# Grouped-query attention by single heads, with the value products two items behind the scores; the depthwise convolution beside the projections

## Chip, cores and metric

One Trainium2 chip, one of its cores. The metric is the device time of one execution in microseconds (us). Everything is float32. TensorE is PE in the profile, VectorE DVE, ScalarE ACT, GpSimd POOL, SyncE SP.

## The reference

One inference step of a two-layer backbone over 512 latent tokens and 128 context tokens (640 rows, width 1024). Layer 0 mixes with an RG-LRU and differential attention, layer 1 with a gated DeltaNet and grouped-query attention; each layer ends in a mixture of 16 experts. The change lies in layer 1:

```python
z = jnp.dot(h, P['w_in_cd'][li])                     # one combined projection
qkv = jax.nn.silu(centred_depthwise_conv(qkv, conv_w))   # 4 taps, 1536 channels
q = rms_norm(qg...); k = rms_norm(kg...)             # 8 query heads, 2 key heads, 64 wide
s = jnp.einsum('bqngd,bknd->bngqk', qb, k) * HEAD_DIM ** -0.5
p = jax.nn.softmax(s, axis=-1)
o = jnp.einsum('bngqk,bknd->bqngd', p, v)
```

Latent tokens attend to 128 cached and 512 own keys (640), context tokens to their own 128.

## The kernel before

The kernel is written by hand for each engine: one program each for PE, ACT, DVE, POOL and SP, with semaphores between them. Each engine runs its program in the order in which it is written. PSUM is used as four pairs of 4 KB banks (1024 floats): `take` makes PE wait until a pair is free, `finish` marks it full, `filled` makes a reader wait for it, and `release` frees it.

Layer 1 goes as follows. PE makes the projection in six chunks (L192): two that give `z2` by rows (queries, keys, values, decay inputs), three that give the convolution's channels transposed into `pad` (four units each, `("pT", 1, c, f)`, of about 8.6 us), and one for the gate. ACT and DVE read these units in turns (`read_T`, L319); between its reads DVE normalises and rotates queries and keys (`gqa_rows_dve`). Then the decay sums follow, the queries and keys are turned (L1645 to L1652), and the attention loop starts (`gqa_pe`, `gqa_act`, `gqa_dve`).

The loop has 20 items, an item being a tile of 128 query rows and a pair of heads m; the first 16 have 640 keys, the last 4 have 128. For each item, e = 0, 1 being the two heads:

- scores on PE (L1667, L1669; L1672 in the small items): each head is 64 rows deep and uses one half of the array's rows; the orders for head 0 and head 1 alternate. Head e writes pair e. A float32 matmul shows as two in the trace.
- maximum on DVE (L1601): one reduction over both heads.
- exponential and its sum on ACT (L1517), one for each head; this frees the pair.
- reciprocal (L1608) and the product with it (L1610) on DVE.
- turn: 10 transposes on PE (L1681) into 1280 columns of pairs 2 and 3, and one copy of them on ACT (L319).
- values: 20 matmuls on PE (L1697) in two halves of the array's columns, into pair 3, and a copy of 128 columns on DVE (L1616).

PE's order is scores(j+2), turn(j+1), rows(j). DVE's is scaled(j+1), maxes(j+2), two or three of the 48 taps of the convolution (`TAPS`, L1631 and L1633), result(j). After the loop ACT runs the convolution's Silu (L2074), and PE turns the convolution's channels (`conv_pe`, L1815 and L1817); the DeltaNet follows.

Of the kernel before, what the change touches and what calls it, by code (L numbers as in the profile page):

```python
# [22 lines left out]
P = 128  # L23
# [55 lines left out]
def build(nc, io, outs):  # L79
    with ExitStack() as ctx:  # L80
# [1387 lines left out]
        upper = PSUM[:, 2:4, :].rearrange("p a b -> p (a b)")  # L1468
        gturn, gres = upper[:, 0:1280], upper[:, 1536:1664]
# [5 lines left out]
        TAPS = [(ct, tap) for ct in range(12) for tap in range(4)]  # L1475
        cv = [hflat[:, UW * i:UW * i + UW] for i in range(3)]
# [27 lines left out]
        def gqa_act(act, step):  # L1504
# [3 lines left out]
            def exps(j):  # L1508
                n = T if GP[j][0] < ST else P
                act.wait_ge(S("g_max"), j + 1)  # L1510
                if j >= 2:
                    filled(act, ("gaT", j - 2))
                if j >= 4:
                    act.wait_ge(S("g_norm"), 2 * (j - 3))
                for e in range(2):
                    u = ("gs", j, e)
                    release(act.activation(gp[j % 2][:, e, 0:n], filled(act, u)[:, 0:n], ACT.Exp, bias=nmax(j, e),  # L1517
                                           accum_out=psum_of(j, e)), u)

            def turned(j):  # L1520
                n = 2 * (T if GP[j][0] < ST else P)
                if j >= 2:
                    filled(act, ("go", j - 2))
                filled(act, ("gaT", j))
                release(copy(act, gaT[j % 2][:, 0:n], gturn[:, 0:n]), ("gaT", j))

            for j in range(-2, len(GP)):
                if j + 2 < len(GP):
                    exps(j + 2)
                if 0 <= j + 1 < len(GP):  # L1530
                    turned(j + 1)
# [53 lines left out]
        def gqa_dve(v, step):  # L1585
            filled(v, ("pR", 1, 3, 2))
            v.wait_ge(S("pad_evac0"), 8)
            v.wait_ge(S("pad_evac1"), 8)
            for c in range(3):
                for f in range(4):  # L1590
                    emptied(v, ("pT", 1, c, f))
# [3 lines left out]
            def maxes(j):  # L1595
                n = T if GP[j][0] < ST else P
                for e in range(2):
                    if j >= 4:
                        emptied(v, ("gs", j - 4, e))
                    filled(v, ("gs", j, e))  # L1600
                v.tensor_reduce(smx[:, 2 * (j % 4):2 * (j % 4) + 2], PSUM[:, 0:2, 0:n], AX_X, ALU.max, negate=True)\  # L1601
# [1019 lines left out]
```

## Time and profile before

| what | value |
|---|---|
| time, median of 3 runs | 1860.54 us (1860.17 to 1864.04) |
| the profiled execution's own time | 1863.33 us |
| its span | 1861.5 us |
| PE busy | 1578.3 us (85%) |
| DVE busy | 647.7 us (35%) |
| ACT busy | 450.9 us (24%) |
| POOL busy | 195.5 us (11%) |
| attention loop, first score to the convolution's turning | 1080.52 to 1177.19 |

Starts are in us from the span's start; a row gives the engine, the line, the tiles written and read, the shape, and the number of instructions merged in it. "Idle before" names what ended the wait.

### The profile page before, as it was taken

The numbers are of one execution on the slowest core, as the hardware profiler recorded it, in microseconds if no ns is written. First come the engines' busy times: TensorE is split into PE (matmuls) and PEld (weight loads), VectorE is DVE, ScalarE is ACT, GpSimd is POOL, SyncE is SP. The second block draws the span as 40 slices with busy tenths as digits, with TensorE's granted clock in tenths as the row PEclk, the third lists the DMA queues.
The fourth block names the chain that finished last, engine by engine and source line by source line (L and its number), as shares of the span: only waits on it lengthen the run. The fifth ranks groups of instructions, "written<-read, shape, count | busy, mean of one in ns | idle before, by whom it ended". The sixth has DMA issues, their size and how long they took to land.

```text
span 1861.5 us, 37187 instructions
## 1 busy us (share of the span) xinstructions
PE 1578.3 (85%) x16388; PEld 1039.3 (56%) x16388; DVE 647.7 (35%) x1284; ACT 450.9 (24%) x746; POOL 195.5 (11%) x197
## 2 busy tenths in 40 slices
PE   5999965778839999995999977688887957999993
PEld 2554433444517677663555456577775536667762
DVE  5134476552270000004044179734453262000003
ACT  4111284441021111103010055532221031111110
POOL 0000000000001111100000000054640001111103
PEclk8999986998969999997999989788988988999997
DMA  9822370455217999994121100000004225999994
GB/s 342 302 91 90 138 280 6 176 202 205 87 67 274 374 389 383 379 354 136 49 86 49 45 1 1 1 2 3 2 3 159 79 102 175 374 371 391 373 396 153
DMA packets 90316, 330.03 MB, mean 177 GB/s; under 512 B 10709, under 2 KB 16457, under 8 KB 82025
## 3 DMA queue, kind: packets, MB, share of 16 engines
q1 hardware_dynamic: 76016, 287.29, 40.6%
q0 software_dynamic: 9168, 32.65, 6.4%
q10 hardware_dynamic: 5032, 8.65, 1.3%
q8 instruction: 77, 1.26, 0.3%
q14 instruction: 23, 0.18, 0.0%
HBM read 303.79 MB, written 24.78 MB: 177 GB/s over the span
## 4 chain that ended last, share of the span: by engine, by line
PE 72%; DVE 12%; DMA 6%; ACT 5%; issue 5%; POOL 0%; ACTq 0%; DVEq 0%; SPq 0%
PE pairs L192 26%; PE pairs L1245 14%; PE pairs L1257 11%; DMA ring<-in_exp_w 3%; PE pairs L1228 2%; DVE sm L1601 1%; PE pairs L1934 1%; PE pairs L1936 1%; PE pairs L1923 1%; ACT arena L319 1%; PE pairs L961 1%; PE pairs L421 1%; PE pairs L1667 1%; ACT arena L1517 1%; PE pairs L1082 1%
## 5 line engine op out<-in xcount | busy, mean ns | idle before, releaser
L192 PE MATMUL pairs<-hT,ring 128*128 128x128 f32 (+1 forms) x1120 | 305.6, 436 | 2.1 <-ACT hT L319 2.1
L319 ACT ACTIVATE arena<-pairs 128x512 f32<-128x512 f32 (+7 forms) x212 | 129.8, 632 | 501.5 <-PE pairs L192 251.0
L192 PEld LDWEIGHTS pairs<-hT,ring 128*128 128x128 f32 x1120 | 170.2, 192 | 138.3 <-issue 136.8
L192 PE MATMUL pairs<-ring,hT 128*128 128x512 f32 (+1 forms) x448 | 177.4, 557 | 0.0
L1245 PEld LDWEIGHTS pairs<-arena 128*64 128x64 f32 x4096 | 145.5, 139 | 15.1 <-issue 15.0
L1245 PE MATMUL pairs<-arena 128*64 128x80 f32 x4096 | 148.3, 235 | 3.3 <-issue 2.3
L1245 PEld LDWEIGHTS pairs<-arena,ring 128*64 128x64 f32 x4096 | 142.9, 137 | 14.2 <-issue 14.2
L1245 PE MATMUL pairs<-arena,ring 128*64 128x80 f32 x4096 | 145.9, 233 | 0.9 <-issue 0.7
L192 PEld LDWEIGHTS pairs<-ring,hT 128*128 128x128 f32 x448 | 85.0, 190 | 92.0 <-issue 89.0
L1311 DVE TENSOR_SCALAR hT<-pairs,arena 80x512 f32<-80x512 f32 x32 | 23.9, 747 | 274.6 <-ACT hT L1287 274.6
L1257 PE MATMUL pairs<-ring,arena 128*80 128x512 f32 x256 | 112.8, 593 | 1.6 <-DMA ring<-in_exp_w 1.6
L1257 PE MATMUL pairs<-arena 128*80 128x512 f32 x256 | 112.6, 593 | 0.6 <-DMA arena<-in_exp_w 0.5
L1307 DVE TENSOR_TENSOR arena<-hT,pairs 128x160 f32<-128x160 f32 x64 | 20.6, 322 | 251.9 <-PE pairs L1245 251.9
L319 DVE COPY arena<-pairs 128x512 f32<-128x512 f32 (+7 forms) x37 | 25.3, 705 | 229.2 <-PE pairs L192 223.4
L1338 POOL DMA_INDIRECT moe_rows<-hT,arena x32 | 45.4, 1420 | 298.3 <-DVE hT L1311 298.3
L1257 PEld LDWEIGHTS pairs<-ring,arena 128*80 128x80 f32 x256 | 37.7, 152 | 64.6 <-issue 64.4
L1287 ACT ACTIVATE hT<-pairs,arena 80x512 f32<-80x512 f32 x32 | 21.8, 683 | 214.2 <-PE pairs L1257 214.2
L1257 PEld LDWEIGHTS pairs<-arena 128*80 128x80 f32 x256 | 37.8, 153 | 63.4 <-issue 63.4
L2334 POOL TENSOR_TENSOR arena<-ring,cst 128x256 f32<-128x256 f32 x60 | 44.0, 745 | 258.8 <-DVE ring L2233 224.0
L421 PE MATMUL pairs<-ring,late 128*32 128x512 f32 x384 | 57.1, 720 | 12.8 <-ACT arena L319 6.5
L1044 DVE SCALAR_TENSOR_TENSOR xT<-pairs,modt,xT 128x512 f32<-128x512 f32 x24 | 18.0, 750 | 141.3 <-PE pairs L192 126.5
L1278 ACT ACTIVATE arena<-pairs 128x640 f32<-128x640 f32 x32 | 22.5, 703 | 183.8 <-PE pairs L1228 183.8
(374 smaller groups left out, 2074.6 us busy)
## 6 DMA issues: line engine op xcount, KB each, us to landing
arena<-in_exp_w SPq DMA_DIRECT2D x48, 2048.0 KB, 19.2
ring<-in_exp_w SPq DMA_DIRECT2D x48, 2048.0 KB, 21.6
ring<-in_w_mod SPq DMA_DIRECT2D x24, 2048.0 KB, 8.0
ring<-in_w_in_ab SPq DMA_DIRECT2D x5, 2048.0 KB, 11.6
ring<-in_w_in_cd SPq DMA_DIRECT2D x5, 2048.0 KB, 8.1
ring<-in_w_out SPq DMA_DIRECT2D x4, 2048.0 KB, 8.0
moe_rows<-arena POOLq DMA_DIRECT2D x2, 2560.0 KB, 15.7
h_rows<-arena POOLq DMA_DIRECT2D x2, 2560.0 KB, 8.4
```

The lines of the kernel that those rows point to most:

```text
L192: last = pe.matmul(out, lhs(k), rhs(k), start=(k == 0), stop=(k == KD - 1))
L319: return eng.activation(dst, src, ACT.Copy) if eng is nc.scalar else eng.tensor_copy(dst, src)
L421: last = pe.matmul(ps[32 * q:32 * q + 32, 0:512], csil[:, k, :], w[:, k, :], start=(j == 0), stop=(j == 1))
L1228: last = pe.transpose(ps[:, o:o + CAP], xe[par][:, k::KD], ident[0:CAP, 0:CAP])
L1245: last = pe.matmul(lin_of(j, f)[c:c + 64, :], w[:, k, f * P + c:f * P + c + 64], rhs, start=(k == 0), stop=(k == KD - 1))
L1257: last = pe.matmul(PSUM[0:CAP, 3, 512 * half:512 * half + 512], hid[par][:, f, :], w2[:, f, 512 * half:512 * half + 512], start=(f == 0), ...
L1278: act.activation(xeT[par], ps, ACT.Copy).then_inc(pair_free[0], 1)
L1287: act.activation(ye[par][:, 0:512], PSUM[0:CAP, 3, 0:512], ACT.Copy, scale=gateT[:, bass.ds(i, 1)])\
L1307: v.tensor_tensor(hid[par][:, f, :], slu[par][:, f, :], lin[1][:, h], ALU.mult)\
L1311: v.tensor_scalar(ye[par][:, 512:1024], PSUM[0:CAP, 3, 512:1024], gateT[:, bass.ds(i, 1)], None, ALU.mult).then_inc(pair_free[3], 1)
L1338: g.indirect_dma_start(DR["m", l], off(e), ye[e % 2], None, compute_op=ALU.add)\
L2334: g.tensor_tensor(am64(j), a64(j), over_heads(C64[f"level{e}{s}"]), ALU.mult).then_inc(S(f"dl_am{e}"), 1)
```

## The change

- The convolution's 48 taps leave the loop: `delta_conv_dve(v, c)` runs 16 of them on DVE after `read_T` of chunk c. Its scratch tiles move from `hT` to the arena.
- The Silu leaves `delta_act`; `delta_silu_act` runs it on ACT after the three chunks' reads.
- Scores, maxima, exponentials and reciprocals go by single heads, `(j, e)`. Scores of head 1 are issued after both matmuls of head 0.
- The product with the reciprocal moves from DVE to POOL (`gqa_pool`).
- PE's order becomes scores(i, 0), scores(i, 1), rows(i-2), turn(i-1, 0), turn(i-1, 1).
- Six of the ten turned blocks go to pair 2 and are copied by ACT (768 columns); four go to the first bank of pair 3 and are copied by DVE (`rest`, 512 columns). The value products have the second bank of pair 3 (`gupper[:, 512:640]`).

```diff
 kdup = ar(20888, NT, 256)
 cdup = ar(22168, 256)
 GP = [(t, m) for t in range(NT) for m in range(4)]
-TAPS = [(ct, tap) for ct in range(12) for tap in range(4)]
-cv = [hflat[:, UW * i:UW * i + UW] for i in range(3)]
...
+def delta_conv_dve(v, c):
+    for part in range(2):
+        v.wait_ge(S("pad_evac" + str(part)), 4 + 2 * c)
+    for f in range(4):
+        emptied(v, ("pT", 1, c, f))
+    for ct in range(4 * c, 4 * c + 4):
+        for tap in range(4):
+            w = cB[:, dw_col + 12 * tap + ct:dw_col + 12 * tap + ct + 1]
+            n_tap = 4 * ct + tap
+            if n_tap:
+                v.wait_ge(S("cv_tap"), n_tap)
+            y, x = cv[ct % 2], pad[:, ct, tap:tap + UW]
+            if tap == 0:
+                v.tensor_scalar(y, x, w, None, ALU.mult).then_inc(S("cv_tap"), 1)
+            else:
+                v.scalar_tensor_tensor(out=y if tap < 3 else pad[:, ct, 0:UW], in0=x, scalar=w, in1=y,
+                                       op0=ALU.mult, op1=ALU.add).then_inc(S("cv_tap"), 1)
+def delta_silu_act(act):
+    for ct in range(12):
+        act.wait_ge(S("cv_tap"), 4 * ct + 4)
+        act.activation(pad[:, ct, 0:UW], pad[:, ct, 0:UW], ACT.Silu).then_inc(S("cv_silu"), 1)
 beta = sm[:, 256:296]
 gdec = sm[:, 296:336]
...
-    def exps(j):
+    def exps(j, e):
         n = T if GP[j][0] < ST else P
-        act.wait_ge(S("g_max"), j + 1)
-        if j >= 2:
+        act.wait_ge(S("g_max"), 2 * j + e + 1)
+        if j >= 2 and e == 1 and GP[j - 2][0] < ST:
+            act.wait_ge(S("g_rest"), j - 1)
+        elif j >= 2:
             filled(act, ("gaT", j - 2))
         if j >= 4:
-            act.wait_ge(S("g_norm"), 2 * (j - 3))
-        for e in range(2):
-            u = ("gs", j, e)
-            release(act.activation(gp[j % 2][:, e, 0:n], filled(act, u)[:, 0:n], ACT.Exp, bias=nmax(j, e),
-                                   accum_out=psum_of(j, e)), u)
+            act.wait_ge(S("g_recip"), 2 * (j - 4) + e + 1)
+        u = ("gs", j, e)
+        release(act.activation(gp[j % 2][:, e, 0:n], filled(act, u)[:, 0:n], ACT.Exp, bias=nmax(j, e),
+                               accum_out=psum_of(j, e)), u)
     def turned(j):
-        n = 2 * (T if GP[j][0] < ST else P)
+        n = 768 if GP[j][0] < ST else 256
         if j >= 2:
-            filled(act, ("go", j - 2))
-        filled(act, ("gaT", j))
-        release(copy(act, gaT[j % 2][:, 0:n], gturn[:, 0:n]), ("gaT", j))
-    for j in range(-2, len(GP)):
-        if j + 2 < len(GP):
-            exps(j + 2)
-        if 0 <= j + 1 < len(GP):
-            turned(j + 1)
+            act.wait_ge(S("g_result"), j - 1)
+        u = ("gaT", j)
+        release(copy(act, gaT[j % 2][:, 0:n], filled(act, u)[:, 256:256 + n]), u)
+    for i in range(len(GP) + 2):
+        if 0 <= i - 2 < len(GP):
+            turned(i - 2)
+        if i < len(GP):
+            exps(i, 0)
+            exps(i, 1)
...
 def gqa_dve(v, step):
-    filled(v, ("pR", 1, 3, 2))
-    v.wait_ge(S("pad_evac0"), 8)
-    v.wait_ge(S("pad_evac1"), 8)
-    for c in range(3):
-        for f in range(4):
-            emptied(v, ("pT", 1, c, f))
     for n in range(2):
         release(v.tensor_copy(gkT[:, n, :], filled(v, ("gkT", n))[:, 0:768]), ("gkT", n))
-    def maxes(j):
+    def maxes(j, e):
+        n = T if GP[j][0] < ST else P
+        if j >= 4:
+            emptied(v, ("gs", j - 4, e))
+        v.tensor_reduce(nmax(j, e), filled(v, ("gs", j, e))[:, 0:n], AX_X, ALU.max, negate=True)\
+            .then_inc(S("g_max"), 1)
+    def recip(j, e):
+        emptied(v, ("gs", j, e))
+        if j >= 4:
+            v.wait_ge(S("g_norm"), 2 * (j - 4) + e + 1)
+        v.reciprocal(rsum(j, e), psum_of(j, e)).then_inc(S("g_recip"), 1)
+    def rest(j):
+        if GP[j][0] < ST:
+            if j >= 2:
+                v.wait_ge(S("g_result"), j - 1)
+            v.wait_ge(S("g_rest"), j + 1)
+            v.tensor_copy(gaT[j % 2][:, 768:1280], gupper[:, 0:512]).then_inc(S("g_rest_read"), 1)
+    def result(j):
+        t, m = GP[j]
+        v.wait_ge(S("g_result"), j + 1)
+        v.tensor_copy(hT[:, 4 + m, t * P:t * P + P], gupper[:, 512:640]).then_inc(S("g_result_read"), 1)
+    for i in range(len(GP) + 3):
+        if 0 <= i - 1 < len(GP):
+            recip(i - 1, 0)
+        if 0 <= i - 2 < len(GP):
+            rest(i - 2)
+        if 0 <= i - 3 < len(GP):
+            result(i - 3)
+        if 0 <= i - 1 < len(GP):
+            recip(i - 1, 1)
+        if i < len(GP):
+            maxes(i, 0)
+            maxes(i, 1)
+def gqa_pool(g):
+    for j in range(len(GP)):
         n = T if GP[j][0] < ST else P
         for e in range(2):
-            if j >= 4:
-                emptied(v, ("gs", j - 4, e))
-            filled(v, ("gs", j, e))
-        v.tensor_reduce(smx[:, 2 * (j % 4):2 * (j % 4) + 2], PSUM[:, 0:2, 0:n], AX_X, ALU.max, negate=True)\
-            .then_inc(S("g_max"), 1)
-    def scaled(j):
-        n = T if GP[j][0] < ST else P
-        for e in range(2):
-            emptied(v, ("gs", j, e))
-        step(v.reciprocal(rsum(j, 0, 2), psum_of(j, 0, 2)))
-        for e in range(2):
-            v.tensor_scalar(gp[j % 2][:, e, 0:n], gp[j % 2][:, e, 0:n], rsum(j, e), None, ALU.mult)\
-                .then_inc(S("g_norm"), 1)
-    def result(j):
-        t, m = GP[j]
-        filled(v, ("go", j))
-        release(v.tensor_copy(hT[:, 4 + m, t * P:t * P + P], gres), ("go", j))
-    for j in range(-2, len(GP)):
-        if 0 <= j + 1 < len(GP):
-            scaled(j + 1)
-        if j + 2 < len(GP):
-            maxes(j + 2)
-        for ct, tap in TAPS[(j + 2) * len(TAPS) // 22:(j + 3) * len(TAPS) // 22]:
-            w = cB[:, dw_col + 12 * tap + ct:dw_col + 12 * tap + ct + 1]
-            n_tap = 4 * ct + tap
-            if n_tap:
-                v.wait_ge(S("cv_tap"), n_tap)
-            c, x = cv[ct % 2], pad[:, ct, tap:tap + UW]
-            if tap == 0:
-                v.tensor_scalar(c, x, w, None, ALU.mult).then_inc(S("cv_tap"), 1)
-            else:
-                v.scalar_tensor_tensor(out=c if tap < 3 else pad[:, ct, 0:UW], in0=x, scalar=w, in1=c,
-                                       op0=ALU.mult, op1=ALU.add).then_inc(S("cv_tap"), 1)
-        if j >= 0:
-            result(j)
+            g.wait_ge(S("g_recip"), 2 * j + e + 1)
+            p = gp[j % 2][:, e, 0:n]
+            g.tensor_tensor(p, p, rsum(j, e).broadcast_to((P, n)), ALU.mult).then_inc(S("g_norm"), 1)
...
-    def scores(j):
+    def scores(j, e):
         t, m = GP[j]
-        ps = [take(pe, ("gs", j, e), e) for e in range(2)]
-        q = [gqT[64 * e:64 * e + 64, m, t * P:t * P + P] for e in range(2)]
-        k = [gkT[64 * e:64 * e + 64, m // 2, :] for e in range(2)]
+        u = ("gs", j, e)
+        ps = take(pe, u, e)
+        r = slice(64 * e, 64 * e + 64)
+        q, k = gqT[r, m, t * P:t * P + P], gkT[r, m // 2, :]
         if t < ST:
-            for e in range(2):
-                pe.matmul(ps[e][:, 0:512], q[e], k[e][:, 0:512], start=True, stop=True)
-            for e in range(2):
-                finish(pe.matmul(ps[e][:, 512:T], q[e], k[e][:, 512:T], start=True, stop=True), ("gs", j, e))
+            pe.matmul(ps[:, 0:512], q, k[:, 0:512], start=True, stop=True)
+            finish(pe.matmul(ps[:, 512:T], q, k[:, 512:T], start=True, stop=True), u)
         else:
-            for e in range(2):
-                finish(pe.matmul(ps[e][:, 0:P], q[e], k[e][:, T:768], start=True, stop=True), ("gs", j, e))
-    def turn(j):
-        pe.wait_ge(S("g_norm"), 2 * j + 2)
+            finish(pe.matmul(ps[:, 0:P], q, k[:, T:768], start=True, stop=True), u)
+    def turn(j, e):
+        nk = NT if GP[j][0] < ST else 1
+        pe.wait_ge(S("g_norm"), 2 * j + e + 1)
         u = ("gaT", j)
-        take(pe, u, 2)
-        nk = NT if GP[j][0] < ST else 1
-        for e in range(2):
-            for b in range(nk):
-                last = pe.transpose(gturn[:, (e * nk + b) * P:(e * nk + b + 1) * P],
-                                    gp[j % 2][:, e, b * P:b * P + P], ident)
-        finish(last, u)
+        ps = take(pe, u, 2) if e == 0 else PSUM[:, 2, :]
+        for b in range(nk):
+            k = e * nk + b
+            if k == 6 and j:
+                pe.wait_ge(S("g_rest_read"), j)
+            out = ps[:, 256 + P * k:384 + P * k] if k < 6 else gupper[:, P * (k - 6):P * (k - 5)]
+            ins = pe.transpose(out, gp[j % 2][:, e, b * P:b * P + P], ident)
+            if k == (5 if nk == NT else 1):
+                finish(ins, u)
+            elif k == 9:
+                ins.then_inc(S("g_rest"), 1)
     def rows(j):
         t, m = GP[j]
         nk = NT if t < ST else 1
-        u = ("go", j)
-        take(pe, u, 3)
+        if j:
+            pe.wait_ge(S("g_result_read"), j)
         emptied(pe, ("gaT", j))
+        if nk == NT:
+            pe.wait_ge(S("g_rest_read"), j + 1)
         o = 64 * (m // 2)
         for b in range(nk):
             vals = z2[:, ST, 656 + o:720 + o] if t == ST else \
                 gv_c[:, o:o + HD] if b == 0 else z2[:, b - 1, 656 + o:720 + o]
             for e in range(2):
-                last = pe.matmul(gres[64 * e:64 * e + 64, :], vals,
+                last = pe.matmul(gupper[64 * e:64 * e + 64, 512:640], vals,
                                  gaT[j % 2][:, (e * nk + b) * P:(e * nk + b + 1) * P], start=(b == 0),
                                  stop=(b == nk - 1))
-        finish(last, u)
+        last.then_inc(S("g_result"), 1)
     pe.wait_ge(pair_free[3], units.uses[3])
-    for j in range(-2, len(GP)):
-        if j + 2 < len(GP):
-            scores(j + 2)
-        if 0 <= j + 1 < len(GP):
-            turn(j + 1)
-        if j >= 0:
-            rows(j)
+    for i in range(len(GP) + 2):
+        if i < len(GP):
+            scores(i, 0)
+            scores(i, 1)
+        if 0 <= i - 2 < len(GP):
+            rows(i - 2)
+        if 0 <= i - 1 < len(GP):
+            turn(i - 1, 0)
+            turn(i - 1, 1)
+    pe.wait_ge(S("g_result_read"), len(GP))
...
 def delta_act(act, step):
-    def silu(ct):
-        act.wait_ge(S("cv_tap"), 4 * ct + 4)
-        act.activation(pad[:, ct, 0:UW], pad[:, ct, 0:UW], ACT.Silu).then_inc(S("cv_silu"), 1)
-    for ct in range(8):
-        silu(ct)
     for c in range(4):
         emptied(act, ("cvT", c))
     act.activation(heads5(qsq), heads4(dq), ACT.Square).then_inc(S("qk_sq"), 1)
-    for ct in range(8, 12):
-        silu(ct)
     for c in range(4, 8):
         emptied(act, ("cvT", c))
     act.activation(heads5(ksq), heads4(dk), ACT.Square).then_inc(S("qk_sq"), 1)
...
@@ -2483,6 +2506,7 @@
             for c in range(3):
                 gqa_rows_act(act, step, c)
                 read_T(act, 1, c, pad[:, 4 * c:4 * c + 4, :], 0, True)
+            delta_silu_act(act)
             read_gate(act, 0)
             filled(act, ("pR", 1, 3, 2))
             decay_act(act)
@@ -2536,6 +2560,7 @@
                 else:
                     gqa_rows_dve(v, step, c)
                 read_T(v, 1, c, pad[:, 4 * c:4 * c + 4, :], 1, True)
+                delta_conv_dve(v, c)
             read_gate(v, 1)
             decay_sums_dve(v, step)
             gqa_dve(v, step)
@@ -2559,6 +2584,7 @@
     route_pool(g, 0)
     moe_pool(g, 0)
     layer1_outputs(g)
+    gqa_pool(g)
     delta_pool(g, step)
     route_pool(g, 1)
     moe_pool(g, 1)
```

## Rows read from the trace of the kernel before

**Rows 1.** The page: its chain, shares by engine.
```profile
PE 72%; DVE 12%; DMA 6%; ACT 5%; issue 5%; POOL 0%; ACTq 0%; DVEq 0%; SPq 0%
```

**Rows 2.** Windows of the loop: stretch, length, busy by engine, granted clock, DMA.
```profile
1080.50:1091.27 10.77, 6.17 (x27) 4.05 (x27) 7.24 (x10) 3.47 (x9) 0.00 (x0) 0.68 0.00 0
...
1115.53:1159.48 43.95, 34.58 (x342) 26.30 (x343) 39.81 (x66) 25.09 (x46) 0.00 (x0) 1.00 0.00 1
...
1168.30:1177.19 8.89, 4.12 (x27) 2.01 (x27) 8.60 (x20) 4.62 (x14) 0.00 (x0) 0.70 0.00 1
```

**Rows 3.** Waits from 1080 to 1177: us in total, times, longest.
```profile
ACT arena L1517 <- DVE sm L1601: 43.4, 19, 5.3
```

**Rows 4.** The critical chain in the loop: start, us, what.
```profile
1080.52 1.13 PE pairs L1667 x4
...
1091.27 1.13 PE pairs L1667 x4
...
1115.53 1.13 PE pairs L1667 x4
...
1117.03 1.50 DVE sm L1601
...
1120.35 1.13 PE pairs L1667 x4
...
1159.48 0.51 PE pairs L1672 x4
```

**Rows 5.** PE's timeline in two items: start, length, line, operation.
```profile
1116.81 1.31 PE L1681 MATMUL pairs<-cst,arena 128*128 128x128 f32 x10
1118.06 0.44 PE L1697 MATMUL pairs<-arena,late 128*64 128x128 f32 x4
...
1165.92 0.44 PE L1697 MATMUL pairs<-arena,late 128*64 128x128 f32 x4
...
1167.16 0.49 PE L1672 MATMUL pairs<-arena 64*128 64x128 f32 x4
```

**Rows 6.** PE's timeline in the projection's last chunk.
```profile
1032.22 34.50 PE L192 MATMUL pairs<-ring,hT 128*128 128x512 f32 x80
```

**Rows 7.** Groups by shape, 960 to 1240 us: count, busy us, mean ns, idle before.
```profile
L1601 DVE TENSOR_REDUCE sm<-pairs 128x2 f32<-128x1280 f32 x16 | 23.9, 1491 | 7.0 <-PE pairs L1669 7.0
...
L1601 DVE TENSOR_REDUCE sm<-pairs 128x2 f32<-128x256 f32 x4 | 1.7, 422 | 0.0
...
L1517 ACT ACTIVATE arena<-pairs,sm 128x640 f32<-128x640 f32 x32 | 25.1, 789 | 38.8 <-DVE sm L1601 38.8
...
L319 ACT ACTIVATE arena<-pairs 128x1280 f32<-128x1280 f32 x16 | 19.8, 1234 | 0.5 <-PE pairs L1681 0.5
...
L1616 DVE COPY hT<-pairs 128x128 f32<-128x128 f32 x20 | 5.7, 285 | 1.3 <-PE pairs L1697 1.3
...
L319 DVE COPY arena<-pairs 128x512 f32<-128x512 f32 x6 | 4.2, 692 | 69.2 <-PE pairs L192 69.2
...
L1633 DVE SCALAR_TENSOR_TENSOR hT<-arena,cB,hT 128x643 f32<-128x643 f32 x24 | 21.2, 884 | 0.4
```

**Rows 8.** Groups by shape on POOL, whole span.
```profile
L2345 POOL TENSOR_TENSOR ring<-arena,sm 128x512 f32<-128x512 f32 x9 | 9.3, 1038 | 15.2 <-PE pairs L1999 12.1 <-PE pairs L1989 3.1
...
L1446 POOL TENSOR_TENSOR arena<-arena,xT 128x1024 f32<-128x1024 f32 x2 | 6.4, 3199 | 0.2
```

**Rows 9.** DVE's timeline beside the projection.
```profile
964.00 2.81 DVE L777 TENSOR_REDUCE sm<-arena 128x40 f32<-128x2560 f32 x1
...
983.87 0.89 DVE L319 COPY arena<-pairs 128x512 f32<-128x512 f32 x2
...
997.81 0.89 DVE L319 COPY arena<-pairs 128x512 f32<-128x512 f32 x2 [13.06 <-PE pairs L192]
```

**Rows 10.** Timeline where the loop ends.
```profile
1175.10 1.28 ACT L2074 ACT_TABLE_LOAD   x1
...
1177.19 1.98 PE L1815 MATMUL pairs<-cst,arena 128*64 128x128 f32 x16 [0.87 <-ACT arena L2074]
```

More of the change, by code:

```diff
@@ L1467, in build @@
         gaT = [ar(20888 + 1280 * i, 1280) for i in range(2)]
-        upper = PSUM[:, 2:4, :].rearrange("p a b -> p (a b)")
-        gturn, gres = upper[:, 0:1280], upper[:, 1536:1664]
+        gupper = PSUM[:, 3, :]
         gscr = ar(18328, NT * 8, HD)
@@ L1473, in build @@
         GP = [(t, m) for t in range(NT) for m in range(4)]
-        TAPS = [(ct, tap) for ct in range(12) for tap in range(4)]
-        cv = [hflat[:, UW * i:UW * i + UW] for i in range(3)]
+        cv = [ar(14232 + UW * i, UW) for i in range(2)]
+        def delta_conv_dve(v, c):
[19 more added lines that the diff above has]
+                act.activation(pad[:, ct, 0:UW], pad[:, ct, 0:UW], ACT.Silu).then_inc(S("cv_silu"), 1)
         beta = sm[:, 256:296]
@@ L1821, in conv_read @@
             u = ("cvT", ct)
-            filled(eng, ("go", len(GP) - 1))
+            eng.wait_ge(S("g_result"), len(GP))
             eng.wait_ge(S("caches"), 80)
@@ L2411, in layer1_ready @@
         def layer1_ready(pe):
-            emptied(pe, ("go", len(GP) - 1))
+            pe.wait_ge(S("g_result_read"), len(GP))
             for b in range(4):
```

## The prediction

> **What bounds the kernel now.** I read the page's chain first: the end is set by PE for 72% of the span and by DVE for 12% [rows 1]. The change touches the projection of layer 1, where PE streams without a gap, and the attention loop, so the question is who sets the loop's pace. In the windows of its steady part PE is busy 34.58 of 43.95 us, DVE 39.81, ACT 25.09, POOL never, and the granted clock is 1.00 [rows 2]. The waits say that ACT's exponentials stood 43.4 us for DVE's maximum [rows 3]. The chain shows the circle: an item's scores start at 1115.53, the maximum of both heads follows at 1117.03 for 1.50 us, then the two exponentials, and the next item's scores start at 1120.35 because both pairs must be free [rows 4]. One round is 4.82 us. It is a latency circle: PE stands idle for about 1 us of it, and DVE fills its gaps with the taps.
>
> From the start of item 2's scores (1091.27) to item 16's (1159.48) there are 14 rounds in 68.2 us, 4.87 each. Before them items 0 and 1 took 10.75 us from 1080.52 [rows 4] at a mean clock of 0.68 [rows 2]. After them, 17.7 us pass from 1159.48 to the first turning of the convolution at 1177.19 [rows 4, 10].
>
> **The change, part by part.** All pieces are put into one round whose time zero is the start of head 0's scores.
>
> *PE.* The turn takes 1.25 us from its start to the start of the values (1116.81 to 1118.06), and the values 1.24 us to the start of the next scores (1165.92 to 1167.16) [rows 5]. Both remain. The scores change. Before, they took 1.28 us (1115.53 to 1116.81) [rows 4, 5]. Alone, one pass over 512 columns takes 34.50 / 80 = 0.431 us [rows 6], so four passes for the two heads would take 1.72 us, and the four short ones of 128 columns 0.43 us: 2.16 us. Before, the heads alternated and ran side by side in the two halves of the array, which is why 1.28 was enough. Now both matmuls of head 0 stand ahead of head 1's first in PE's order, and they use the same half. I count 2.16 us, plus 0.15 for the start and the change of shape (1.28 exceeds half of 2.16 by 0.20; the estimate keeps most of it), less 0.11 for head 1's first pass beside head 0's last: 2.2 us. The sum of PE's round is 2.2 + 1.24 + 1.25 = 4.69 us. Bounds: 3.8 if the heads still ran side by side, 4.9 if nothing overlaps and each further semaphore costs something.
>
> The row shows four passes and the short ones in 1.28 us when the heads alternate [rows 4, 5], less than four times the 0.431 us of a pass [rows 6]. The Trainium skill (TensorE: Matmul & The Clock Gate, Part 3: Packing small matmuls, The mechanism) says that matmuls keep program order and only those in other row groups overlap. By it the new order gives the 2.2 us; were it not so, 1.28 would stay and the round would be 3.8 us. This rule speaks against the new order.
>
> *DVE.* Two maxima of 640 columns: the rows at 1280 and 256 columns differ by 1069 ns for 1024 columns [rows 7], so one is 0.82 us. Copying 512 columns of the turn takes 0.69, the result 0.285 [rows 7], and two reciprocals a little: with 0.3 for these, 2.9 us a round. The two multiplications and the taps (48 of them, 0.884 us for most [rows 7], some 38 us in all) are gone. DVE no longer sets the pace.
>
> *ACT.* Two exponentials at 0.79 each, and a copy that shrinks from 1280 columns, 1.23 us [rows 7], to 768, some 0.8: 2.4 us. Not the pace.
>
> *POOL.* A product of 640 columns with a broadcast factor. The nearest row is 1038 ns for 512 columns with a broadcast operand, so 1.30 us; with two full operands it is 3199 ns for 1024, so 2.0 us [rows 8]. I take 1.30, since the operand is broadcast here too. Two are 2.6 us a round (4.0 at most), below 4.69. POOL would set the pace from 2.35 us for one.
>
> The multiplication on DVE was cheaper than on POOL. The Trainium skill (GPSIMD Engine Reference, 3.1 Elementwise — side-by-side cycle accounting) measures 4497 ns for 2048 columns of two operands; by it one product is an estimated 1.4 us and a round's two are 2.8 us. It speaks against the move, but changes no sum here.
>
> *Does PE find everything ready?* Head 0's scores end at 1.1 and head 1's at 2.2. The maxima run from 1.3 to 2.1 and from 2.4 to 3.2, the exponentials from 2.2 to 3.0 and from 3.3 to 4.1. The next round starts at 4.69, and both pairs are free: the circle that set 4.82 is down to about 3.1 for each head. The values of item i-2 start at 2.2; their blocks were turned by time 0 and copied by ACT and DVE by about 1.0. The latest piece is the product of head 1: its reciprocal waits on DVE behind `rest` and `result` until 1.3, POOL multiplies until about 2.8, and PE wants it at 2.2 + 1.24 + 0.62 = 4.06. That is 1.3 us of slack, 0.6 with the dearer product. So I take the steady round as PE's 4.69: 14 x (4.87 - 4.69) = 2.5 us gained. With the bounds 3.8 and 4.9 it is from 15 us gained to 0.4 lost.
>
> *Start of the loop.* Head 0's first exponential ends at 3.0 and head 1's at 4.1; scores of item 1 fill 3.1 to 5.4, the turn of item 0 follows, and item 2 starts at 6.9, if the clock is full. With half the clock from the second item on, which the 0.68 suggests [rows 2], it is 9.8. Gain 0.9 to 3.9 us; I take 1.0, the clock being as before.
>
> *End of the loop.* Item 16's round still holds a full value product and turn: 3.4 us with a wait for the last full product. The next waits for the copies of that turn, 1.1, then 1.24 and 0.3: 2.65. Two rounds of small items follow at about 1.6 and 1.8, then the last product, its turn, copy, values and result: about 4.0. That is 13.4 us with the 0.70 clock of this stretch [rows 2] in mind, against 17.7: 4.3 gained (3 to 5.5). In it is ACT's table load and first Silu, which PE waited 0.87 us for [rows 10]; the new wait for the last result costs about 0.5 in its place.
>
> *The convolution beside the projection.* PE is busy without a break there [rows 6], and DVE mostly waits for it: 13.06 us before one read [rows 9]. 16 taps are 12.8 us. Chunk 0's taps start at 964.0, where the query rows' work began, and that work (964.00 to 983.87 [rows 9]) then ends at 997. DVE's first read of chunk 1 slips from 983.87 to 997. The pair it frees is wanted again only three units after it was filled, at about 1006 (filled by 980.5, each unit 8.6 us by 34.50 / 4 [rows 6]). Cover: 9 us. Chunk 1's taps run from 998.7 to 1011.5 and delay the keys' rows to about 1023, while PE projects until 1066.7; chunk 2's end by 1046, when the gate's first unit fills (two of five tiles of the 34.50 us from 1032.22 [rows 6]). ACT's 12 Silus go under the same cover. Cost: nothing; if a chunk's taps took over 22 us the surplus would be paid by PE.
>
> *After the loop.* The turning of the convolution is paced by PE and DVE's copies as before. No gain, no loss, except for the clock.
>
> **Sum.** 1.0 + 2.5 + 4.3 = 7.8 us. The profiled execution took 1863.33 us (span 1861.5), 2.8 over the median 1860.54; taken from the median the forecast is 1852.7 us.
>
> **Rivals.**
>
> *The heads overlap after all.* PE's round is then 3.8, and the other engines' longest circle is below it. For it: they did overlap; against: the order. 14 x 1.07 + 5.3 = 20 us gained: about 1840. Chance 0.06.
>
> *Nothing gained in the steady part.* PE's round is 4.87 or more, because the serial scores, changes of shape and added waits eat the idle 1 us. For it: my 4.69 is only 0.18 below what is there. Only start and end are left, 5.3 us or less: 1855 to 1860. Chance 0.20, of which half lies within 0.2%.
>
> *POOL sets the pace (the slower side).* From 2.35 us a product POOL is the bound. Against: 1.04 us for 512 columns [rows 8]. At twice the broadcast row's rate, 2.6 us, a round is 5.4 with the hand-overs: 16 x 0.53 = 8.5 lost against 5.3 gained, 1864; with more, later. Chance 0.05.
>
> *The taps stall the projection.* DVE frees a pair too late and PE stands still. Against: 9 us of cover. Were a chunk's taps to take twice their 12.8 us, 4 us beyond the cover would be lost in each of two chunks, and the whole comes to about no change, 1861. Chance 0.03.
>
> **How the numbers follow.** The forecast has 0.66, its own range 1848 to 1857, from the start's 0.9 to 3.9, the round between 4.6 and 4.8 and the end's 3 to 5.5. The range of 8 in 10 reaches into the second rival and some way toward the first: 1845 to 1859. 0.2% is 3.7 us, about what a measurement of this kernel can tell from no change. Faster: 0.66 + 0.06 + 0.10 = 0.82; within: 0.10 + 0.03 = 0.13; slower: 0.05.
>
> **What the new profile would show.** Scores of a full item last about 2.2 us from start to the start of the values; the steady round is 4.6 to 4.8 us with PE busy over 95% of it; ACT's wait for the maximum no longer lengthens the round; POOL's products are about 1.3 us; DVE has the taps between 964 and 1047, and the projection ends at 1066.8 as before; the loop starts at 1080.5 and the turning of the convolution at about 1169. I would be wrong if the products took over 2.35 us, if scores took 1.3 us, or if PE showed gaps before L192 or before the turn.

## The result and the profile after

The changed kernel takes 1843.8 us (median of 4 executions, 1838.64 to 1847.48) against 1862.3 us for the kernel before in the same comparison. The ratio is 0.990 with a 95% interval of 0.987 to 0.993: 18.5 us less. The forecast was 1852.7 us with a range of 1845 to 1859, so the direction was right and the gain more than twice the 7.8 us foretold.

The profiled execution took 1838.64 us, the fastest of the four, and its span is 1836.1 us, 25.4 less than that of the profile before. Where they lie:

| stretch | before | after | difference |
|---|---|---|---|
| span's start to the projection's end | 1066.8 | 1064.3 | -2.5 |
| projection's end to the first score | 13.8 | 11.5 | -2.3 |
| first score to item 2's scores | 10.8 | 8.7 | -2.0 |
| 14 full rounds, items 2 to 15 | 68.2 | 55.2 | -13.0 |
| item 16's scores to the convolution's turning | 17.7 | 12.6 | -5.2 |
| from there to the span's end | 684.3 | 683.8 | -0.5 |

The first line holds the projection beside which the taps now run, but the projection takes 177.3 us in both kernels (889.45 to 1066.72 before, 886.96 to 1064.23 after), so its 2.5 us lie ahead of it. In the second line the mean clock differs: 0.83 from 1060 to 1080.5 before, 1.00 from 1060 to 1075.75 after. This stretch took 11.4 to 13.8 us in the kernels below, and 11.6 in b_scores_by_head, whose program is the old one there. So I read the change as the loop's 20.2 us, which agrees with the 18.5 of the medians.

The windows of the changed kernel, with the columns of [rows 2]:

```profile
1075.75:1084.49 8.74, 6.95 (x28) 4.85 (x28) 3.60 (x7) 3.97 (x9) 3.71 (x3) 0.71 0.00 0
...
1100.00:1134.00 34.00, 34.00 (x335) 27.32 (x335) 23.15 (x53) 20.38 (x44) 22.14 (x18) 1.00 0.01 2
...
1143.39:1152.27 8.88, 6.42 (x58) 3.98 (x57) 4.55 (x20) 4.41 (x17) 2.79 (x7) 0.94 0.00 1
```

PE is busy in all 34.00 us of the middle window, where it was busy 34.58 of 43.95 [rows 2]. DVE has fallen from 39.81 of 43.95 to 23.15 of 34.00. The chain, set out like [rows 4], now stays on PE through whole rounds:

```profile
1104.67 1.16 PE pairs L1689 x4
1105.83 0.36 PE pairs L1690 x3
1106.19 1.24 PE pairs L1726 x20
1107.44 1.24 PE pairs L1706 x10
1108.68 1.07 PE pairs L1689 x4
...
1109.97 1.24 PE pairs L1726 x20
1111.21 1.24 PE pairs L1706 x10
1112.45 1.16 PE pairs L1689 x4
```

L1689 and L1690 are the scores, L1726 the values, L1706 the turn. Values and turn take 1.24 us each, as foretold. The scores take 1.52 and 1.29 us in turns, not 2.2, and the rounds 4.00 and 3.77 us. Both kinds stand in PE's timeline:

```profile
1112.38 1.37 PE L1689 MATMUL pairs<-arena 64*128 64x512 f32 x4
...
1113.34 0.63 PE L1690 MATMUL pairs<-arena 64*128 64x128 f32 x4
...
1113.90 0.44 PE L1726 MATMUL pairs<-arena,late 128*64 128x128 f32 x4
...
1116.39 1.14 PE L1689 MATMUL pairs<-arena 64*128 64x512 f32 x4
...
1117.35 0.40 PE L1690 MATMUL pairs<-arena 64*128 64x128 f32 x4
...
1117.68 0.44 PE L1726 MATMUL pairs<-arena,late 128*64 128x128 f32 x4
```

Four passes over 512 columns in 1.14 us can't be one behind the other: a single one takes 0.431 [rows 6]. In the longer kind head 1's first pass starts 0.25 us after head 0's, because its pair was still in use: the second exponential of the item before ends 0.20 us after head 0's start. The groups by shape give the pieces, as in [rows 7]:

```profile
L1658 POOL TENSOR_TENSOR arena<-arena,sm 128x640 f32<-128x640 f32 x32 | 40.0, 1252 | 85.8 <-DVE sm L1625 85.8
...
L1541 ACT ACTIVATE arena<-pairs,sm 128x640 f32<-128x640 f32 x32 | 25.1, 790 | 29.2 <-DVE sm L1618 29.2
L1618 DVE TENSOR_REDUCE sm<-pairs 128x1 f32<-128x640 f32 x32 | 25.0, 819 | 8.6 <-PE pairs L1690 8.6
...
L319 ACT ACTIVATE arena<-pairs 128x768 f32<-128x768 f32 x16 | 12.9, 807 | 1.2 <-PE pairs L1706 1.2
```

The forecast had 1.30 for the product on POOL, 0.82 for a maximum, 0.8 for the copy; they are 1.25, 0.82 and 0.81.

Beside the projection, DVE's timeline (first row) and PE's (second):

```profile
1041.73 2.74 DVE L1492 SCALAR_TENSOR_TENSOR arena<-arena,cB 128x643 f32<-128x643 f32 x3
```
```profile
1029.73 34.50 PE L192 MATMUL pairs<-ring,hT 128*128 128x512 f32 x80
```

The last taps end at about 1044.4, when DVE begins to read the gate's first unit, and the last chunk still takes 34.50 us [rows 6], the whole projection still 177.3: the taps cost the projection nothing.

### The profile page after: what moved, and what is told of

Same layout as the page of the kernel before. It is cut to its first block, busy times and chain, and to the rows that moved or that the text cites. A ratio compares the mean times of both kernels' runs of the same rounds, so it can differ in the third digit from the quotient of the medians.

```text
span 1836.1 us, 37283 instructions
## 1 busy us (share of the span) xinstructions
PE 1571.6 (86%) x16388; PEld 1039.0 (57%) x16388; DVE 645.6 (35%) x1300; ACT 444.5 (24%) x746; POOL 238.5 (13%) x237
## 4 chain that ended last, share of the span: by engine, by line
PE 75%; DVE 11%; DMA 6%; issue 4%; ACT 4%; POOL 0%; ACTq 0%; DVEq 0%; SPq 0%
PE pairs L192 26%; PE pairs L1245 14%; PE pairs L1257 11%; DMA ring<-in_exp_w 3%; PE pairs L1228 2%; PE pairs L1965 1%; PE pairs L1967 1%; PE pairs L421 1%; PE pairs L1706 1%; PE pairs L1726 1%; PE pairs L1954 1%; PE pairs L1689 1%; PE pairs L961 1%; ACT arena L319 1%; PE pairs L1082 1%
## 5 line engine op out<-in xcount | busy, mean ns | idle before, releaser
L319 ACT ACTIVATE arena<-pairs 128x512 f32<-128x512 f32 (+6 forms) x212 | 122.8, 600 | 452.3 <-PE pairs L192 201.6
L1245 PEld LDWEIGHTS pairs<-arena,ring 128*64 128x64 f32 x4096 | 142.7, 137 | 13.8 <-issue 13.8
L192 PEld LDWEIGHTS pairs<-ring,hT 128*128 128x128 f32 x448 | 84.8, 190 | 92.2 <-issue 89.1
L421 PE MATMUL pairs<-ring,late 128*32 128x512 f32 x384 | 53.0, 674 | 14.6 <-ACT arena L319 5.9
L501 ACT ACTIVATE arena<-xT 128x640 f32<-128x640 f32 x32 | 23.4, 736 | 154.6 <-DVE xT L1047 135.2
## 6 DMA issues: line engine op xcount, KB each, us to landing
ring<-in_w_in_ab SPq DMA_DIRECT2D x5, 2048.0 KB, 11.5
```

The lines of the kernel that those rows point to most:

```text
L192: last = pe.matmul(out, lhs(k), rhs(k), start=(k == 0), stop=(k == KD - 1))
L319: return eng.activation(dst, src, ACT.Copy) if eng is nc.scalar else eng.tensor_copy(dst, src)
L421: last = pe.matmul(ps[32 * q:32 * q + 32, 0:512], csil[:, k, :], w[:, k, :], start=(j == 0), stop=(j == 1))
L501: act.activation(sq_all[:, k, :] if (l, n) == (1, 0) else sq[:, k % 2, :], xT[:, k, :], ACT.Square).then_inc(S("sq"), 1)
L1245: last = pe.matmul(lin_of(j, f)[c:c + 64, :], w[:, k, f * P + c:f * P + c + 64], rhs, start=(k == 0), stop=(k == KD - 1))
```

## The experiments

All loops below are measured in the profile from the first score to the first turning of the convolution. "Round" is the usual length of a full round; two numbers alternate. Ratios are to the kernel before.

| kernel | round, us | loop, us | median, us | ratio (95%) |
|---|---|---|---|---|
| before | 4.82 | 96.7 | 1862.3 | 1 |
| changed | 3.77, 4.00 | 76.5 | 1843.8 | 0.990 (0.987 to 0.993) |
| b_scores_by_head | 4.84 | 97.6 | 1864.6 | 1.001 (0.999 to 1.003) |
| a_one_half | 4.84 | 94.7 | 1859.3 | 0.998 (0.996 to 0.999) |
| a_three_blocks | 4.30 | 85.0 | 1848.5 | 0.992 (0.989 to 0.995) |
| a_five_blocks | 4.57 | 89.1 | 1851.5 | 0.995 (0.993 to 0.996) |
| b_conv_beside | 4.82 | 93.1 | 1861.3 | 1.000 (0.998 to 1.001) |
| b_conv_and_pool | 5.56 | 109.3 | 1874.1 | 1.006 (1.004 to 1.008) |
| a_heads_alone | 4.96, 5.30 | 102.5 | 1864.7 | 1.002 (1.000 to 1.004) |
| a_taps_in_loop | 3.89, 4.23 | 85.7 | 1853.7 | 0.995 (0.993 to 0.996) |
| a_product_dve | 3.94, 4.02 | 78.3 | 1841.6 | 0.988 (0.986 to 0.991) |
| a_product_twice | 4.84 | 92.8 | 1858.4 | 0.998 (0.997 to 0.999) |
| a_values_last | 3.81, 4.12 | 78.3 | 1840.1 | 0.989 (0.986 to 0.992) |
| a_result_first | 3.77, 4.01 | 76.2 | 1842.4 | 0.989 (0.987 to 0.991) |

Names with b_ start from the kernel before, those with a_ from the changed one. Medians of one comparison run some 2 us beside those of another (the kernel before had 1861.9 to 1863.8), so the ratios and the loops carry the argument.

**What do the scores cost in the new order?**

b_scores_by_head:

```diff
                     for e in range(2):
                         pe.matmul(ps[e][:, 0:512], q[e], k[e][:, 0:512], start=True, stop=True)
-                    for e in range(2):
                         finish(pe.matmul(ps[e][:, 512:T], q[e], k[e][:, 512:T], start=True, stop=True), ("gs", j, e))
```

> The kernel before, with head 1's scores issued only after both matmuls of head 0; nothing else. Theory A (the two halves of the array run side by side whatever the order of issue): scores still 1.28 us from their start to the turn's, round 4.82 us, time unchanged within 2 us. Theory B (the premise of the prediction: this order makes the heads run one behind the other): scores 2.2 us, the circle of 4.82 us grows by 0.9, and 16 rounds cost 14 us more.

PE's timeline has the scores from 1113.66 to the turn at 1114.95, 1.29 us, as before:

```profile
1113.66 1.14 PE L1667 MATMUL pairs<-arena 64*128 64x512 f32 x4 [0.63 <-ACT arena L1517]
1114.59 0.42 PE L1668 MATMUL pairs<-arena 64*128 64x128 f32 x4
1114.95 0.77 PE L1680 MATMUL pairs<-cst,arena 128*128 128x128 f32 x5
```

Theory A holds: the loop is 0.9 us longer and the median 0.8. The premise of the forecast, that this order makes the heads run one behind the other, is false already on the kernel before.

a_one_half (head 1's scores come from head 0's rows, so the attention output differs from the reference's):

```diff
-                r = slice(64 * e, 64 * e + 64)
+                r = slice(0, 64)
```

> The changed kernel, with head 1's scores taken from head 0's rows, so that both heads need the same half of the array (its attention output is therefore not the reference's). Both theories: the scores can't overlap, 2.2 us, and PE's round becomes the 4.69 us of the prediction. Theory A: the round goes from 3.9 to 4.7 us, 14 rounds cost 11 us, time near 1855 us. Theory B: nothing changes, since the heads were serial already and the gain came from elsewhere.

```profile
1120.07 1.12 PE L1689 MATMUL pairs<-arena 64*128 64x512 f32 x2
1121.03 0.38 PE L1690 MATMUL pairs<-arena 64*128 64x128 f32 x2
1121.25 1.02 PE L1689 MATMUL pairs<-arena 64*128 64x512 f32 x2
1122.11 0.38 PE L1690 MATMUL pairs<-arena 64*128 64x128 f32 x2
1122.42 0.44 PE L1726 MATMUL pairs<-arena,late 128*64 128x128 f32 x4
```

Now the heads do follow one another: 2.35 us from 1120.07 to 1122.42, and the round is 4.84. Theory A, but at a higher price than expected: the loop is 18.2 us longer than the changed kernel's, 17.1 in the 14 full rounds where 11 were foretold. Of these 4.5 lie in the first round alone (9.22 against 4.68 us), which ran at a granted clock of 0.50 here and of 0.80 in the changed kernel. This is the world that the forecast described; its 4.69 was 0.15 low, and the kernel is 4.5 us faster than before by the medians.

a_five_blocks and a_three_blocks ask how far behind head 1 may stand:

```diff
-                    pe.matmul(ps[:, 0:512], q, k[:, 0:512], start=True, stop=True)
-                    finish(pe.matmul(ps[:, 512:T], q, k[:, 512:T], start=True, stop=True), u)
+                    for b in range(NT):
+                        last = pe.matmul(ps[:, b * P:b * P + P], q, k[:, b * P:b * P + P], start=True, stop=True)
+                    finish(last, u)
```

> The changed kernel with each head's scores in five matmuls of 128 columns in place of one of 512 and one of 128: ten short passes of head 0 stand ahead of head 1's first. Theory A (PE lets the other half of the array start however far behind it stands in the order): scores 1.3 to 1.6 us, round 3.9 us, no change within 2 us. Theory C (it looks only a few passes ahead): head 1 starts late, scores 1.8 to 2.3 us, round 4.4 to 4.8 us, 7 to 12 us lost.

```profile
1109.77 2.16 PE L1690 MATMUL pairs<-arena 64*128 64x128 f32 x20
...
1111.86 0.44 PE L1727 MATMUL pairs<-arena,late 128*64 128x128 f32 x4
```

The scores take 2.09 us for the same columns, and the round 4.57: theory C. By the single starts in the trace, head 1's first pass starts 0.78 us after head 0's first, when seven of head 0's ten passes have started. With one matmul of 512 and one of 128 it starts at once, when one of four has. In both, three passes of head 0 had not started. Its pair is not what it waits for: the exponential that frees it ended 0.56 us ahead of head 0's first pass. The first full round, at a granted clock of 0.50, took 8.53 us, and the loop is 12.6 us longer than the changed kernel's. The next kernel takes 256, 256 and 128 columns, six passes:

```diff
-                    pe.matmul(ps[:, 0:512], q, k[:, 0:512], start=True, stop=True)
+                    pe.matmul(ps[:, 0:256], q, k[:, 0:256], start=True, stop=True)
+                    pe.matmul(ps[:, 256:512], q, k[:, 256:512], start=True, stop=True)
```

> The changed kernel with each head's scores in matmuls of 256, 256 and 128 columns: six passes of head 0 ahead of head 1's first. In the two kernels so far head 1 started when three passes of head 0 had not started. If that is the rule here (theory C): head 1 starts with head 0's third pass, 0.45 us in, scores 1.7 us, every full round 4.2 to 4.25 us, 4 to 5 us lost. Rival (the look-ahead goes by columns or by time, and 640 columns lie within it as before): head 1 starts at once, round 3.9 us, nothing lost.

```profile
1111.33 0.70 PE L1689 MATMUL pairs<-arena 64*128 64x256 f32 x2
1111.86 0.38 PE L1690 MATMUL pairs<-arena 64*128 64x256 f32 x1
1111.87 0.48 PE L1689 MATMUL pairs<-arena 64*128 64x256 f32 x1
...
1112.29 0.38 PE L1691 MATMUL pairs<-arena 64*128 64x128 f32 x2
1112.40 0.59 PE L1690 MATMUL pairs<-arena 64*128 64x256 f32 x2
1112.83 0.38 PE L1691 MATMUL pairs<-arena 64*128 64x128 f32 x2
1113.14 0.44 PE L1727 MATMUL pairs<-arena,late 128*64 128x128 f32 x4
```

L1689 is the first block, L1690 the second, L1691 the last. Head 0's two passes of L1689 come at 1111.33, its third pass at 1111.86, and head 1's first at 1111.87, ahead of three of head 0's that stand before it in the program. Here too the pair was free, 0.33 us ahead of head 0's first pass. The scores take 1.81 us and the round is 4.30, 0.05 above the range. The rule of three held; the sum of the loss did not. The loop is 8.5 us longer than the changed kernel's where 4 to 5 were foretold, 3.2 of it in the first full round (7.84 against 4.68 us), at a granted clock of 0.52.

**Which part gains?**

b_conv_beside: `delta_conv_dve` and `delta_silu_act` in the kernel before, the taps out of its loop.

```diff
-                for ct, tap in TAPS[(j + 2) * len(TAPS) // 22:(j + 3) * len(TAPS) // 22]:
...
+                        delta_conv_dve(v, c)
...
+                    delta_silu_act(act)
```

> The kernel before with the convolution's taps and Silu beside the projection and nothing else of the change. Theory A (the circle of both heads sets the round): 14 rounds fall from 4.87 to 4.80 us at most, since the taps lay in DVE's gaps, and what is gained is at the loop's end, where taps stood ahead of the results, and in the Silu: 4 to 6 us in all, time 1857 to 1860 us. Rival (the taps were the load): rounds near 4.4 us, 8 us or more gained.

The round stays 4.82. The loop is 3.6 us shorter in the profile, all of it behind the full rounds (13.7 us from item 16's scores on, against 17.7). The medians show nothing of it: 1861.3 against 1861.9, where 1857 to 1860 was expected. The rival is out: the taps did lie in gaps of a circle that they didn't set.

b_conv_and_pool adds the product on POOL, with both heads together:

```diff
-                step(v.reciprocal(rsum(j, 0, 2), psum_of(j, 0, 2)))
-                for e in range(2):
-                    v.tensor_scalar(gp[j % 2][:, e, 0:n], gp[j % 2][:, e, 0:n], rsum(j, e), None, ALU.mult)\
-                        .then_inc(S("g_norm"), 1)
+                if j >= 4:
+                    v.wait_ge(S("g_norm"), 2 * (j - 3))
+                v.reciprocal(rsum(j, 0, 2), psum_of(j, 0, 2)).then_inc(S("g_recip"), 1)
```

> The kernel before with the convolution beside the projection and the product on POOL, but with both heads together and the old order on PE. DVE is relieved as in the changed kernel. Theory A (relieving DVE is not enough; the heads' circle and the order decide): the two products take 2.5 us behind the reciprocal and PE wants them 1.3 us after it, so the turn starts about 2.9 us into the round and the round is 2.9 + 1.25 + 1.24 = 5.4 us; 8 to 10 us slower than before. Rival (DVE's load set the pace): round 4.4 us or less, faster than before by 7 us.

```profile
1105.08 1.13 PE L1685 MATMUL pairs<-arena 64*128 64x512 f32 x4
...
1105.64 2.46 POOL L1654 TENSOR_TENSOR arena<-arena,sm 128x640 f32<-128x640 f32 x2 [3.10 <-DVE sm L1632]
...
1108.16 1.31 PE L1699 MATMUL pairs<-cst,arena 128*128 128x128 f32 x10 [1.73 <-POOL arena L1654]
```

PE stands 1.73 us for POOL in each round, the turn starts 3.1 us after the scores, and the round is 5.56: slower than before by 0.6%, a little more than expected. DVE is relieved, but in the old order PE waits for POOL's product, and that costs time.

a_heads_alone is the other half: single heads and the new order, with taps, Silu and product where they were (its two edits are those of the next two kernels).

> The changed kernel with the taps and the Silu back in the loop and the product back on DVE: single heads and the new order alone. DVE has 2.9 + 1.1 + 1.9 = 5.9 us of work for a round by the rows of one instruction, some 5.2 where instructions overlap. Theory A (DVE must be relieved first): round 5.0 to 5.6 us, slower than before by 0 to 8 us. Rival (single heads are what gains, whatever DVE carries): round 4.4 us, 6 us or more faster than before.

Rounds of 4.96 and 5.30 us, loop 102.5 us, 1.002: no faster. Over 80 us of its loop the windows have DVE busy for 77.97:

```profile
1090.00:1170.00 80.00, 66.61 (x594) 51.13 (x590) 77.97 (x158) 35.80 (x80) 0.00 (x0) 0.98 0.01 1
```

a_taps_in_loop puts only the taps and the Silu back:

```diff
-                        delta_conv_dve(v, c)
...
-                    delta_silu_act(act)
...
+                for ct, tap in TAPS[i * len(TAPS) // 22:(i + 1) * len(TAPS) // 22]:
...
```

> The changed kernel with the 48 taps and the Silu back where they were, in DVE's loop. DVE's round is then 2.9 us plus 2.2 taps of 0.85, 4.8 us. If the convolution's move matters (theory A): round 4.7 to 4.9 us, nearly the whole gain is lost, time 1857 to 1862 us. Rival: the taps fit in the idle time of DVE (about 1.2 us a round), round 4.1 to 4.3 us, 4 to 6 us lost.

The loop is 9.1 us longer: 4.0 in the 14 full rounds and 5.1 after them, where DVE still has taps between the small items' work and the Silu stands ahead of the turning. The rounds are those of the rival, the loss that of neither: I had counted rounds alone and left out the loop's end. DVE is busy 49.17 us of 50 here.

a_product_dve puts only the product back:

```diff
                 v.reciprocal(rsum(j, e), psum_of(j, e)).then_inc(S("g_recip"), 1)
+                v.wait_ge(S("g_recip"), 2 * j + e + 1)
+                n = T if GP[j][0] < ST else P
+                v.tensor_scalar(gp[j % 2][:, e, 0:n], gp[j % 2][:, e, 0:n], rsum(j, e), None, ALU.mult)\
+                    .then_inc(S("g_norm"), 1)
...
-            gqa_pool(g)
```

> The changed kernel with the product with the reciprocal back on DVE, behind each reciprocal. DVE's round is 4.0 us, and the maxima start some 0.6 us later behind rest, result and the second product, so that head 1's exponential is late: round 4.3 to 4.5 us, 5 to 8 us lost, time near 1850 us. Rival: POOL's 1.25 us against DVE's 0.55 in the chain to the turn gives it back; no change within 2 us.

The rival: 3.94 and 4.02 us, 1.8 us more in the loop, nothing in the medians. With the taps gone, DVE had room for it (46.22 of 50 us busy). So the product's move to POOL is no needed part of the gain: this kernel's ratio is 0.988 without it, the changed kernel's 0.990 with it.

**How near are the other circles?**

a_product_twice makes each product once more into free space:

```diff
+                    g.tensor_tensor(hflat[:, 0:n], p, rsum(j, e).broadcast_to((P, n)), ALU.mult)\
+                        .then_inc(S("g_extra"), 1)
```

> The changed kernel with each product made twice on POOL, once into free space. POOL then has 4 x 1.25 = 5.0 us a full round and is the bound: round 5.1 to 5.4 us, 18 to 22 us lost against the changed kernel, time 1862 to 1866 us. Rival (POOL lies beside the path with room to spare): under 5 us lost.

POOL is busy 50.00 of 50.00 us and the round is 4.84, four products of 1.21. The mechanism was right. The loss is 16.3 us in the loop and 15 in the medians, where 18 to 22 were foretold; the rounds were to be 5.1 to 5.4, but products that follow one another take 1.21 and not 1.25 us, and nothing is added to them.

a_values_last issues the values behind the turn:

```diff
             if i < len(GP):
                 scores(i, 0)
                 scores(i, 1)
-            if 0 <= i - 2 < len(GP):
-                rows(i - 2)
             if 0 <= i - 1 < len(GP):
                 turn(i - 1, 0)
                 turn(i - 1, 1)
+            if 0 <= i - 2 < len(GP):
+                rows(i - 2)
```

> The changed kernel with rows(i-2) issued behind turn(i-1) in place of ahead of it. Theory A (the values two items behind cover the product): PE reaches the turn of head 1 at 1.26 + 0.62 = 1.9 us of the round, and POOL's product ends at about 2.5 us by the trace of the changed kernel, so the round becomes 4.4 to 4.6 us, 8 us lost. Rival (the pipeline shifts by itself and finds the same pace): under 2 us lost.

Rounds of 3.81 and 4.12, loop 1.8 us longer, nothing in the medians: the rival. The pipeline shifts: `rest` starts 0.8 us ahead of the next scores in place of 0.2 behind their start, and head 1's reciprocal 0.3 behind it in place of 1.0, since the turn ends 1.24 us sooner. That the values stand just there isn't what gains.

a_result_first swaps two calls on DVE:

```diff
+                if 0 <= i - 3 < len(GP):
+                    result(i - 3)
                 if 0 <= i - 2 < len(GP):
                     rest(i - 2)
-                if 0 <= i - 3 < len(GP):
-                    result(i - 3)
```

> The changed kernel with DVE's result(i-3) ahead of rest(i-2). In the full rounds nothing waits for it: no change. At the loop's end PE stood 0.6 us each for the result in items 16 and 17 and the copy of rest goes out at the same time: 0.3 us gained in each of 2 or 3 items, under 1 us in all, which the times can't show and the timeline can.

The loop is 76.2 against 76.5 us, and rounds 16 and 17 are 0.1 us shorter each, where 0.3 was expected; the times can't tell it from the changed kernel.

## Why the prediction was wrong, by its own steps

**PE's scores: the step that failed.** I counted 2.2 us because both matmuls of head 0 stand ahead of head 1's in the order. They measured 1.29 and 1.52, and scores of 1.3 us were one of the signs that the forecast gave for being wrong. The two halves of the array ran side by side whether the orders alternated or not (b_scores_by_head), and only when both heads needed the same half did they cost 2.35 (a_one_half). The Trainium skill (TensorE: Matmul & The Clock Gate, Part 3: Packing small matmuls, The mechanism) says that matmuls start in program order; here they don't: in a_three_blocks head 1's first pass starts ahead of three earlier ones of head 0, and it is late only by what stands beyond those three. The trace of before already held a hint: I looked at the sum of its four passes, 1.13 us, and not at which started when. Two windows of its PE timeline show it:

```profile
1115.53 0.70 PE L1667 MATMUL pairs<-arena 64*128 64x512 f32 x2 [0.63 <-ACT arena L1517]
...
1116.04 0.62 PE L1667 MATMUL pairs<-arena 64*128 64x512 f32 x2
```

Two passes start together and two more half a microsecond later. One pass takes 0.431 us, so two that start together are in different halves: the first two are one of each head, and head 1's went ahead of head 0's second. That whole matmuls are passed over as well, the row could not show, since there the heads alternate; b_scores_by_head is the first kernel that does.

**The steady round.** With 2.2 it was 4.69; it is 3.77 and 4.00. This is nearly the whole error: 14 rounds gained 13.0 us in place of 2.5. The rival that named it had 20 us at a chance of 0.06. Its round of 3.8 holds in every other item; in the rest, head 1's circle (scores, two maxima, second exponential) is 0.25 us late. The forecast gave each head's circle about 3.1 us. With both heads' scores ready together, their maxima and exponentials queue, and head 1's took 3.95 us, from 1116.40 to 1120.35. That is more than PE's own 3.77, and so every other round is 4.00.

**The circle of the kernel before.** Right: 4.82 was a circle of both heads. Taking the taps away leaves it at 4.82 (b_conv_beside), and of the kernels here only single heads without the full load on DVE shorten it. That the parts need each other the forecast did not say: heads alone 1.002, relief alone 1.000 and 1.006, together 0.990.

**The other engines.** Their prices were right to 0.05 us. POOL had slack as counted; a_product_twice shows the bound where it is reached.

**Start and end.** Forecast 1.0 and 4.3 gained, measured 2.0 and 5.2. The mean clock at the start was 0.71, as before (0.68 [rows 2]). The scores of item 1 took less than two heads in a row would: 3.2 us (1078.89 to 1082.10), against 4.56 (1084.33 to 1088.89) in a_one_half, where the heads follow one another. At the end, the rounds of items 16 and 17 took 3.60 and 2.74 us, 3.4 and 2.65 by the forecast; what came after took 6.2 in place of 7.4. The clock was 0.94 in the last 8.9 us, where it was 0.70 before [rows 2] and in the forecast. How much of the gain at the end is the clock's is not shown.

**The convolution beside the projection.** Right: no cost, 177.3 us before and after. That most of the taps' worth lay at the loop's end (5.1 us) and only 4.0 in the full rounds was not separated in the forecast.

**Chances.** 0.06 for the case that came was too low: that head 1 would wait for both matmuls of head 0 rested on one rule and no row.

## What to carry to other kernels

A circle through several engines is shortened only where nothing else fills its engines: cutting the item in two and taking the taps off DVE each gave nothing by the times, both together gave 20 us in the loop. In these float32 kernels, work for two halves of PE's array needs no writing in alternation, as long as no more than three passes of the first half stand unstarted ahead of the second's; with many short matmuls per head it does matter (4.57 us a round against a mean of 3.89). And before a sum is built on a rule of order, look up the single starts in the trace at hand.

## What the runs showed that was not expected

- PE starts a matmul for the other half of the array past three unstarted passes of the first: 0.01, 0.54 and 0.78 us behind the first start with four, six and ten passes ahead of it. Whether the three are counted in passes of float32 or in whole matmuls can't be told from these kernels alone.
- The same 640 columns take 1.29 us in two matmuls a head, 1.81 in three and 2.09 in five, all else equal.
- The loop's first full round differs among the kernels, and its granted clock with it: 4.79 us at 1.00 in the kernel before and 4.68 at 0.80 in the changed one, but 6.79 at 0.53 in b_scores_by_head and 7.84, 8.53 and 9.22 at 0.52, 0.50 and 0.50 in a_three_blocks, a_five_blocks and a_one_half. What lowers the clock there is not shown.
- Each change of the array's shape in the loop costs about 0.09 us: from the last start of a group to the first of the next it is 0.20 us, against 0.11 within a group. It is 0.20 without a semaphore wait between as well (L1846 to L1848 of the changed kernel). Not every change costs it: from 128x128 to 128x16 (L1089 to L1103) it is 0.11.
